# First attention of a two-block kernel: the scores of two heads in one step, rotary products on the two halves of the array

## What is computed

```python
def mla_mixer(n, k_nope, k_rope, v, w_dq, q_norm_g, w_uq, w_o, cos, sin):
    q = (rms_norm(n @ w_dq, q_norm_g) @ w_uq).reshape(b, s, N_HEADS, QK_NOPE + QK_ROPE)
    q_nope = q[..., :QK_NOPE]
    q_rope = apply_rope(q[..., QK_NOPE:], cos[:, :, None, :], sin[:, :, None, :])
    for blk in range(s // Q_BLOCK):
        q0, q1 = blk * Q_BLOCK, (blk + 1) * Q_BLOCK
        sc = (jnp.einsum('bqhd,bkhd->bhqk', q_nope[:, q0:q1], k_nope[:, :q1])
              + jnp.einsum('bqhr,bkr->bhqk', q_rope[:, q0:q1], k_rope[:, :q1]))
        ...
        p = jax.nn.softmax(sc, axis=-1).astype(v.dtype)
        outs.append(jnp.einsum('bhqk,bkhd->bqhd', p, v[:, :q1]))
    o = jnp.concatenate(outs, axis=1).reshape(b, s, N_HEADS * V_DIM)
    return o @ w_o
```

## Time and profile before

| | us |
|---|---|
| median of 3 executions | 1350.85 |
| lowest, highest | 1350.75, 1351.29 |
| the profiled execution, its own time | 1352.27 |
| its span | 1350.50 |
| TensorE busy | 1341.3 |
| VectorE busy | 995.4 |
| ScalarE busy | 876.7 |

### The profile page before, as it was taken

One profiled execution on the slowest core, in us unless ns is written; L12 is line 12 of the kernel. 1 busy time (PEld: TensorE's weight loads), 2 busy tenths in 40 slices (PEclk: granted clock), 3 DMA queues, 4 the chain that ended last, 5 costly groups with the idle time before them and its releaser, 6 DMA issues.

```text
span 1350.5 us, 19946 instructions
## 1 busy us (share of the span) xinstructions
PE 1341.3 (99%) x6248; PEld 1113.3 (82%) x6248; DVE 995.4 (74%) x1820; ACT 876.7 (65%) x1624; POOL 49.8 (4%) x86
## 2 busy tenths in 40 slices
PE   9999999999999999999999999999999999999999
PEld 7888888888888888888888888888887888888887
DVE  6777766766887777787776679777767756697774
ACT  6666666645866666666666677666666675676663
POOL 1000010000000001000001010000002000000000
PEclk9999999999999999999999999999999999999999
DMA  8676636665566664666663347655556654566651
GB/s 293 208 229 217 212 120 206 211 205 166 187 217 193 211 196 132 211 199 211 195 212 101 111 140 248 204 187 186 172 149 188 197 172 140 154 222 197 197 192 66
DMA packets 196501, 251.57 MB, mean 186 GB/s; under 512 B 17922, under 2 KB 134880, under 8 KB 196448
## 3 DMA queue, kind: packets, MB, share of 16 engines
q1 hardware_dynamic: 196176, 250.86, 58.4%
q0 software_dynamic: 224, 0.03, 0.0%
q10 hardware_dynamic: 48, 0.02, 0.0%
HBM read 249.80 MB, written 1.05 MB: 186 GB/s over the span
## 4 chain that ended last, share of the span: by engine, by line
PE 95%; DVE 2%; ACT 1%; DMA 1%; issue 1%; POOL 1%; SPq 0%; DVEq 0%; ACTq 0%
PE ps L2005 30%; PE ps L2007 30%; PE ps L2006 30%; PE ps L2031 2%; DMA h<-in_x 0%; PE ps L2307 0%; DMA arena<-in_gmlp_b_s 0%; PE ps L2659 0%; PE ps L2487 0%; PE ps L2488 0%; ACT whi L622 0%; SPq L346 0%; DVE wlo L1262 0%; PE ps L2334 0%; POOL arena L584 0%
## 5 line engine op out<-in xcount | busy, mean ns | idle before, releaser
L2005 PE MATMUL ps<-whi,kthi 128*128 128x512 f32 (+2 forms) x1384 | 542.4, 392 | 1.5 <-DVE wlo L1259 1.1
L2007 PE MATMUL ps<-whi,ktlo 128*128 128x512 f32 (+2 forms) x1384 | 536.4, 388 | 0.0
L2006 PE MATMUL ps<-wlo,kthi 128*128 128x512 f32 (+2 forms) x1384 | 536.0, 387 | 0.0
L1259 DVE SCALAR_TENSOR_TENSOR wlo<-raw,gcol,whi 128x512 fp32r<-128x512 f32 x592 | 412.2, 744 | 148.8 <-ACT whi L622 148.7
L622 ACT ACTIVATE whi<-raw,gcol 128x512 fp32r<-128x512 f32 x592 | 391.3, 714 | 138.3 <-PE ps L2007 135.8
L2005 PEld LDWEIGHTS ps<-whi,kthi 128*128 128x128 f32 x1384 | 259.9, 188 | 55.9 <-issue 1.6
L2007 PEld LDWEIGHTS ps<-whi,ktlo 128*128 128x128 f32 x1384 | 259.8, 188 | 53.4
L2006 PEld LDWEIGHTS ps<-wlo,kthi 128*128 128x128 f32 x1384 | 260.0, 188 | 50.7
L1267 DVE TENSOR_TENSOR wlo<-raw,whi 128x1024 fp32r<-128x1024 f32 x140 | 166.0, 1222 | 41.0 <-ACT whi L626 40.6
L626 ACT CAST whi<-raw 128x1024 fp32r<-128x1024 f32 x140 | 140.8, 1047 | 25.8 <-PE ps L2007 25.8
L2005 PE MATMUL ps<-whi,hthi 128*128 128x512 f32 x400 | 156.1, 390 | 0.0
(11 more groups left out here) (246 smaller groups left out, 831.8 us busy)
## 6 DMA issues: line engine op xcount, KB each, us to landing
raw<-in_ffn_w_gate SPq DMA_DIRECT2D x176, 256.0 KB, 3.6
raw<-in_ffn_w_up SPq DMA_DIRECT2D x176, 256.0 KB, 4.3
raw<-in_ffn_w_down SPq DMA_DIRECT2D x160, 256.0 KB, 3.4
raw<-in_w_in SPq DMA_DIRECT2D x80, 256.0 KB, 3.7
raw<-in_gmlp_w_in SPq DMA_DIRECT2D x64, 256.0 KB, 3.4
raw<-in_w_gate SPq DMA_DIRECT2D x44, 256.0 KB, 3.4
raw<-in_w_up SPq DMA_DIRECT2D x44, 256.0 KB, 4.1
raw<-in_w_down SPq DMA_DIRECT2D x40, 256.0 KB, 3.5
```

The lines of the kernel that those rows point to most:

```text
L1259: ins = nc.vector.scalar_tensor_tensor(out=wlo[:, s, cut], in0=raw[:, s, cut], scalar=gcol[:, k:k + 1], in1=f32(whi[:, s, cut]), op0=ALU.m ...
L2005: nc.tensor.matmul(dst, lhs[0], rhs[0], start=first, stop=False)
L2006: nc.tensor.matmul(dst, lhs[0], rhs[1], start=False, stop=False)
L2007: return nc.tensor.matmul(dst, lhs[1], rhs[0], start=False, stop=last)
```

## The change

The scores of heads i and i + 1 are made in one step, for even i. First come the four products without rotation, then the four rotary ones, each with the 64 rows of its own head: rows 0 to 63 of `qrt` and of the key for the even head, rows 64 to 127 for the odd one. They go to banks 4 and 5 in turn. The key is kept once, `krt`, with the same 64 values in both halves (the turned pair of copies gives that), so the clears and one of two copies fall away. A head's `mla_scores_full` is given with its last rotary product. A pair waits until both heads of the pair before are masked. The orders of VectorE and ScalarE in the attention stay as they are. For the second attention (`fox`) nothing changes but the place of the semaphore's increment.

```diff
-        krt2 = view(12800, 2, S)
+        krt = view(12800, S)
...
-            for e in range(2):
-                own = slice(64 * e, 64 * e + 64)
-                nc.scalar.copy(krt2[own, e, :], ps[own, 7, 0:S]).then_inc(sem("krt_ready"), 1)
+            nc.scalar.copy(krt, ps[:, 7, 0:S]).then_inc(sem("krt_ready"), 1)
...
-            for e in range(2):
-                nc.vector.memset(krt2[64 - 64 * e:128 - 64 * e, e, :], 0.0).then_inc(sem("krt_ready"), 1)
...
-                        pe.wait_ge(sem("krt_ready"), 4)
+                        pe.wait_ge(sem("krt_ready"), 1)
...
                 for i in range(H + 3):
-                    if i < H:
+                    if i < H and i % together == 0:
                         if i >= 2:
 
-                            pe.wait_ge(sem(kind + "_masked"), i - 1)
-                        scores(i).then_inc(sem(kind + "_scores_full"), 1)
+                            pe.wait_ge(sem(kind + "_masked"), i - 2 + together)
+                        scores(i)
...
             def mla_scores(i):
-                bank = ps[:, 4 + i % 2, :]
-                if i % 2 == 0:
-                    pe.wait_ge(sem("qnt_ready"), i // 2 + 1)
+
+                pe.wait_ge(sem("qnt_ready"), i // 2 + 1)
                 if i == 4:
                     pe.wait_ge(sem("qrt_ready"), 2)
+
+                def block(e, t):
+                    bank = ps[:, 4 + e, :]
+                    return bank[:, 0:P] if t == 0 else bank[:, P:3 * P], slice(t * P, (t + 1) * P), slice(0, (t + 1) * P)
+
+                for e in range(2):
+                    for t in range(TT):
+                        dst, q, keys = block(e, t)
+                        nc.tensor.matmul(dst, qnt[:, i + e, q], knt[:, i + e, keys], start=t == 0, stop=False)
                 for t in range(TT):
-                    dst = bank[:, 0:P] if t == 0 else bank[:, P:3 * P]
-                    keys, q = slice(0, (t + 1) * P), slice(t * P, (t + 1) * P)
-                    nc.tensor.matmul(dst, qnt[:, i, q], knt[:, i, keys], start=True, stop=False)
-                    ins = nc.tensor.matmul(dst, qrt[:, i // 2, q], krt2[:, i % 2, keys], start=False, stop=True)
-                return ins
+                    for e in range(2):
+                        dst, q, keys = block(e, t)
+                        own = slice(64 * e, 64 * e + 64)
+                        ins = nc.tensor.matmul(dst, qrt[own, i // 2, q], krt[own, keys], start=False, stop=t == TT - 1)
+                        if t == TT - 1:
+                            ins.then_inc(sem("mla_scores_full"), 1)
...
-            attention("mla", mla_scores, mla_output, p_sb, "mla_p_ready", pt_sb, mla_out)
+            attention("mla", mla_scores, mla_output, p_sb, "mla_p_ready", pt_sb, mla_out, together=2)
```

More of the change, by code:

```diff
@@ L2453, in _, with attention @@
             q_nope(0, 1, lambda: turn_queries(0))
-            def attention(kind, scores, output, probs, probs_ready, turned_probs, filler):
+            def attention(kind, scores, output, probs, probs_ready, turned_probs, filler, together=1):
                 def turn_probs(i):
@@ L2659, in fox_scores @@
                     ins = nc.tensor.matmul(dst, qpad[:, i, t * P:(t + 1) * P], kpad[:, i, 0:(t + 1) * P], start=True, stop=True)
-                return ins
+                ins.then_inc(sem("fox_scores_full"), 1)
             def fox_output(i, pt):
```

## The result

| | median us | lowest, highest | profiled execution: span |
|---|---|---|---|
| before | 1351.20 | 1350.75, 1352.43 | 1350.5 |
| after | 1354.90 | 1354.45, 1355.98 | 1353.4 |

A forecast was written before the change was run, and what follows sets the result against it. TensorE, busy 1341.3 of 1350.5 us, was taken as the bound, with short waits on VectorE. Lateness of 0.75 + 0.85 + 1.05 + 1.05 = 3.7 us on 1350.85 gave 1354.55, said as 1354.6, range 1353.0 to 1356.4.

The forecast's parts named there:

- two waits that lost their cover: Ahead of the projection's first and third row units: TensorE waits some 1.3 us each, heads 5 and 7 being done already.
- The 1.05 us for the rotary block: A pair's 64-row rotary products, switching included, take 1.05 us in place of 1.31.
- Rival 1: Rotary halves of a pair run one after the other: 5.4 us slower, 1356.3; chance 0.06.
- The first term: First pair: masking of head 0, then VectorE's weights and TensorE's product at 750.72, come 0.75 us late.
- The copy and the scores behind it keep their distance: Behind the turning of the rotated queries, copy and scores (760.16) move along unchanged, 1.60 us late.
- The third and fourth term: Pairs of heads 4-5 and 6-7: outputs of heads 1 and 3, and the row units behind, each add 1.05 us.
- The other way of counting: Over the attention, waits grow by 4.7 us and TensorE's work falls by 1.0, so 3.7 remain.
- The signs: Trace checks: masking of head 0 near 748.6, wrong if before 748.3; four longer TensorE waits; later turning near 784.8.
- The masked-wait of two heads: A pair's wait for two masked heads in place of one: claimed to decide nothing, masking one head taking 0.76 us.
- Rival 2: Going in and out of the 64-row form costs nothing: 2.5 us slower, 1353.4; chance 0.12.
- Rival 3: TensorE catches up in the layers behind, paced by the weight stream: no change, 1350.9; chance 0.05.
- Rival 4: Only TensorE's own work counts and the four waits don't grow: 1.0 us less, 1349.9; chance 0.05.

The follow-up runs named there:

- single_64rows: Kernel before, one head a step, but each head's rotary products with its own 64 rows, behind its two others: 1353.36 us, ratio 1.0013.
- before_lows_split: Kernel before with VectorE's low parts ahead of masking head 0 and the later queries' rotation split in two halves: 1350.84 us, ratio 0.9998.
- pairs_late: The change with heads 0 to 3 one by one as before and only heads 4 to 7 in packed pairs: 1353.58 us, ratio 1.0014.
- pairs_padded: The change with rotary products summing over 128 zero-padded rows, so no 64-row form: 1355.55 us, ratio 1.0031.
- rotary_first: The change with a pair's rotary products ahead of its products without rotation: 1354.00 us, ratio 1.0020.
- chains_pairs: Kernel before with low parts first, split rotation, an earlier ScalarE query copy, and packed pairs for heads 0-1, 2-3, 5-6: 1349.89 us, ratio 0.9991.

## Why the prediction was right

The time was forecast at 1354.6 in a range of 1353.0 to 1356.4; the median is 1354.9. The mechanism is right too, later completion and two waits that lost their cover. Term by term, as the time from the first score product (746.26 before, 745.54 after):

| event | before | after | later | forecast |
|---|---|---|---|---|
| masking of head 0 starts | 1.61 | 2.47 | 0.86 | 0.75 |
| second half of the rotary queries | 4.46 | 5.31 | 0.85 | 0.75 |
| masking of head 2 starts | 7.47 | 9.18 | 1.71 | 1.60 |
| turning of the rotated queries | 12.42 | 14.12 | 1.70 | 1.60 |
| scores of head 4 | 13.90 | 15.55 | 1.65 | 1.60 |
| output of head 1 (L2499, L2504) | 18.92 | 21.57 | 2.65 | 2.65 |
| row unit 0 | 20.75 | 23.40 | 2.65 | 2.65 |
| turning of head 6's probabilities | 34.87 | 38.54 | 3.67 | 3.70 |

- **The price of a pair.** 745.54 to the rotary block at 746.94 is 1.40 us, and from 753.76 to the turning at 754.62 it is 0.86. The 1.05 us for the rotary block, read from the retention, holds for the first pair, behind which a three-pass product stands; the other three pairs have a turning behind them, and there it is 1.00, because coming out costs 0.05 less. The two halves run together in the other order of issue as well (two heads' eight passes take 0.93 us with the length of the last one, where one head's four take 0.92 in single_64rows). Rival 1, halves one after the other, is out.
- **The first term was mis-sized by 0.1.** Masking of head 0 came 1.07 us after the start of the rotary block, that of head 2 only 0.96 (753.76 to 754.72), the number of the earlier trace rows. Before, too, head 0 was 0.1 us slower to be masked than head 2, 1.61 against 1.51 us after its start. I had taken the slower one for before and the quicker one for after. The 0.1 is there in all seven traces in which the masking of head 0 is the first thing that VectorE does in the attention; what makes it was not looked into.
- **"The copy and the scores behind it keep their distance"** was right within 0.05 us, but for a reason I had not seen: before, the scores of head 4 waited for a queue of three copies; after, the rotation is so late that ScalarE stands idle for 0.99 us ahead of the third copy, and it starts as soon as TensorE has turned the queries. That gives 0.05 back. before_lows_split brought the queue to light. The line of the trace after:

```profile
760.36 0.59 ACT L1007 COPY arena<-ps 128x512 f32<-128x512 f32 x1 [0.99 <-PE ps L2442]
```

- **The third and fourth term** measured 1.00 and 1.02 us in place of 1.05 each, and pairs_late shows them apart from the rest (2.04 together). The operand of row unit 0 was there 0.1 us ahead of TensorE in the earlier trace rows; a wait of 1.1 us stands there now. By the distance from the last turning to the row unit it is 1.39 us, where it was 0.08.
- **Some luck in the sum.** The first term is 0.10 too small; the copy gives 0.05 back and the last two terms fall short by 0.05 and 0.03. So the sum agrees within 0.03 us, which is closer than its terms do.
- **The other way of counting** holds as well: by the distances of starts the four waits grew by 1.10, 1.14, 1.31 and 1.31 us (forecast 1.0, 1.1, 1.3, 1.3) and the one ahead of head 4's scores shrank by 0.06, 4.8 in all; with 3.67 lost in the end, TensorE's work fell by 1.1.
- **The signs** were given as times of the trace of before, and one of them, a masking of head 0 ahead of 748.3, reads as broken: it started at 748.01. But this attention began 0.72 us earlier; with that added it is 748.73, and the turning forecast near 784.8 is at 784.80. The span, 1353.4 where 1354.2 was forecast, is short by the same early start.
- **The masked-wait of two heads** decided nothing: in no kernel does a score product wait for VectorE.
- **Rival 2** (switching is free, 2.5 us) is out by single_64rows: 0.39 us a head. The Trainium skill's span model (TensorE: Matmul & The Clock Gate, "Measured speedup vs the span model") agrees with this case on the halves running side by side; it has no term for going in and out, and here the measured 0.39 us decides.
- **Rival 3** (the time comes back later) is out by the distance to the end, 604.2 and 607.9 us.
- **Rival 4** (only TensorE's work counts) is out by pairs_padded, which does the work of before in pairs and loses 4.35 us, and by rotary_first, which does the work of the change and loses 1.0 less.

One step of the working was shaky although it came out right: the 0.3 us at the rotation in before was counted as a wait that grows to 1.4. Its removal gains nothing by itself (before_lows_split), a later TensorE can't use it up (single_64rows), and in the sum of waits it stood for the queue of copies behind it. The sum by lateness, which follows each event, did not need it.

## What to carry to other kernels

Where an engine is 99% busy, look at its rare waits and at the waits that are missing by a tenth of a microsecond, and ask of every grouping two things: when is the *first* member of the group complete for the engine that waits for it, and what stood between two dependent steps that the group has now taken away. Here the group saved 1.1 us of work and added 4.8 us of waits. Part of that saving can be had (0.36 us in chains_pairs) by placing the groups where nobody waits for their first member and by giving the waited-for step a place further ahead in the other engine's order. The order was worth more than the form: the exchange of two lines on VectorE gave 0.45 us in the kernel before and 1.5 in the change, three packed pairs gave 0.36 beside shortened chains, and the 64-row form 0.68 where the heads were paired anyway.

## What the runs showed of the hardware

- Going into the 64-row form and out of it costs 0.39 us around a block of float32 products, at a granted clock of 1.00 (single_64rows: a head takes 1.70 us in place of 1.31), and 0.34 where a turning follows. A pair of heads saves 0.65 us of streaming, of which 0.26 is left, or 0.31 ahead of a turning; with a single head the form only costs.
- A float32 product of 64 rows takes as long as one of 128, apart from the switches: 0.22 us for 128 columns, 0.43 for 256. Two of them on the two halves overlap in full, issued turn about or one head after the other (0.93 us for two heads' block, 0.92 for one's).
- A wait in the list can be free. In before the rotation ended 0.3 us after TensorE was ready for it; taking it away changed nothing, since a second chain through ScalarE ended at the same moment.
